# Down product of a feed-forward layer by seven block products, in a fused two-block Trainium2 kernel

## What is computed

```python
def conv_glu_ffn(h, w_up, conv_w, conv_b, w_down):
    u = causal_dwconv(h @ w_up, conv_w) + conv_b
    a, b = jnp.split(u, 2, axis=-1)
    return (jax.nn.silu(a) * b) @ w_down          # 1024x2816 by 2816x1024
...
        y = memory_cross_attention(rmsnorm(h, g[2]), ...)
        h = h + rmsnorm(y, g[3])
        y = conv_glu_ffn(rmsnorm(h, g[4]), ...)
        h = h + rmsnorm(y, g[5])
...
        mod = jax.nn.silu(c) @ w_ada[layer] + b_ada[layer]
        shift, scale, gate = jnp.split(mod[:, None, :], 3, axis=-1)
        h = rms_norm(x, norm_g[layer]) * (1.0 + scale) + shift
        proj = h @ w_in[layer]
```

## Time and profile before

| | us |
|---|---|
| three executions: median (lowest, highest) | 2670.04 (2668.05, 2671.69) |
| the profiled execution | 2670.99 |
| its span, first to last instruction | 2669.2 |
| PE busy | 2591.1 (97%) |
| DVE busy | 1659.6 (62%) |
| POOL busy | 1131.9 (42%) |
| ACT busy | 844.0 (32%) |

### The profile page before, as it was taken

How to read it: one execution, slowest core, us unless ns; L and a number is a source line. 1 busy time by engine, 2 the same in 40 slices (tenths; PEclk the granted TensorE clock), 3 DMA queues, 4 the chain that set the end, 5 groups by cost and what they waited for, 6 DMA issues and landing times.

```text
span 2669.2 us, 33144 instructions
## 1 busy us (share of the span) xinstructions
PE 2591.1 (97%) x13218; PEld 2174.4 (81%) x13218; DVE 1659.6 (62%) x2194; ACT 844.0 (32%) x1332; POOL 1131.9 (42%) x651
## 2 busy tenths in 40 slices
PE   6999899989999999999999999999999999999998
PEld 5788788877788777888888887888888888888887
DVE  4879978766512587666674558804555556476566
ACT  4011233334223433333332436212222222343342
POOL 2433100046632548777754444673223322242364
PEclk9999999999999999999999999999999999999999
DMA  4122333235312412222245553573333342466682
GB/s 153 56 94 97 99 124 127 95 104 206 112 62 79 158 58 86 79 87 79 87 149 191 169 178 121 186 258 106 134 111 111 130 147 94 159 251 211 223 315 111
DMA packets 147381, 360.25 MB, mean 135 GB/s; under 512 B 15173, under 2 KB 51229, under 8 KB 147100
## 3 DMA queue, kind: packets, MB, share of 16 engines
q1 hardware_dynamic: 65072, 177.81, 19.9%
q10 hardware_dynamic: 82156, 180.33, 18.9%
HBM read 268.90 MB, written 89.19 MB: 134 GB/s over the span
## 4 chain that ended last, share of the span: by engine, by line
PE 89%; DVE 4%; POOL 2%; ACT 2%; issue 1%; DMA 1%; ACTq 0%; POOLq 0%; DVEq 0%
PE pp L296 32%; PE pp L2213 13%; PE pp L494 11%; PE pp L2266 9%; PE pp L278 9%; PE pp L2953 2%; PE pp L1272 2%; POOL w_lo L3653 1%; PE pp L1944 1%; PE pp L1983 1%; POOL w_hi L3651 1%; DMA w_raw<-in_weights 1%; PE pp L1558 1%; PE pp L1597 1%; PE pp L444 1%
## 5 line engine op out<-in xcount | busy, mean ns | idle before, releaser
L3651 POOL CAST w_hi<-w_raw 128x1024 fp32r<-128x1024 f32 x184 | 222.2, 1207 | 990.3 <-PE pp L296 659.5
L296 PE MATMUL pp<-w_hi,act_hi 128*128 128x512 f32 x1344 | 535.9, 399 | 12.7 <-POOL w_lo L3653 9.9
L296 PE MATMUL pp<-w_lo,act_hi 128*128 128x512 f32 x1344 | 524.5, 390 | 0.0
L296 PE MATMUL pp<-w_hi,act_lo 128*128 128x512 f32 x1344 | 524.5, 390 | 0.0
L3653 POOL TENSOR_TENSOR w_lo<-w_raw,w_hi 128x1024 fp32r<-128x1024 f32 x184 | 468.9, 2549 | 14.7
L296 PEld LDWEIGHTS pp<-w_hi,act_hi 128*128 128x128 f32 x1344 | 253.0, 188 | 67.9 <-POOL w_lo L3653 10.8
L296 PEld LDWEIGHTS pp<-w_hi,act_lo 128*128 128x128 f32 x1344 | 252.6, 188 | 53.5
L296 PEld LDWEIGHTS pp<-w_lo,act_hi 128*128 128x128 f32 x1344 | 253.2, 188 | 48.3
L494 PE MATMUL pp<-act_hi,w_hi 128*128 128x512 f32 x480 | 192.7, 402 | 10.6 <-DVE act_lo L849 6.5
L2184 POOL TENSOR_TENSOR w_lo<-w_raw,w_hi 128x1024 fp32r<-128x1024 f32 x52 | 132.5, 2550 | 164.7 <-ACT w_hi L2178 164.6
L494 PE MATMUL pp<-act_lo,w_hi 128*128 128x512 f32 x480 | 190.5, 397 | 0.0
(11 more groups left out here) (468 smaller groups left out, 5282.9 us busy)
## 6 DMA issues: line engine op xcount, KB each, us to landing
w_raw<-in_weights SPq DMA_DIRECT2D x314, 512.0 KB, 3.5
z_s<-hg_st ACTq DMA_DIRECT2D x52, 512.0 KB, 4.1
hid_s<-ffn_cb ACTq DMA_DIRECT2D x22, 512.0 KB, 2.6
ffn_graw<-hid_s ACTq DMA_DIRECT2D x44, 256.0 KB, 3.1
hg_qkb<-hT_s SPq DMA_DIRECT2D x16, 512.0 KB, 8.1
qkvT_s<-mixin_o ACTq DMA_DIRECT2D x12, 512.0 KB, 2.8
gdn_qkv<-qkvT_s ACTq DMA_DIRECT2D x8, 768.0 KB, 6.4
front_x<-in_x ACTq DMA_DIRECT2D x8, 512.0 KB, 5.0
```

Of the source, the lines that this page charges most:

```text
L296: last = pe.matmul(dst, a[:, k, t * P:(t + 1) * P], columns(w, j, k, 0, n), start=(k == 0 and a is high and w is w_hi), stop=(k == NK - 1 ...
L3651: pool.tensor_copy(hi, raw).then_inc(w_split, 1)
```

## The change

The down product is now done on 2x2 blocks. The tokens are halved (rows of A), the 22 strips of the hidden dimension go in 11 pairs (columns of A, rows of B), and the 1024 columns of the weight are halved. In place of eight block products there are seven, some of them of sums: T1 to T4 of weight blocks, S1 to S4 of hidden blocks. Each takes 11 steps of 12 matmuls (now L2381), 77 steps in all.

```diff
-FCHUNKS = ((0, 1, 2, 3), (4, 5, 6, 7))
-N_DOWN = len(FCHUNKS) * FG
+DOWN = (("A11", "B11"), ("A12", "B21"), ("S2", "T2"), ("S1", "T1"), ("S4", "B22"), ("S3", "T3"), ("A22", "T4"))
+DOWN_HALVES = (FG + 1) // 2
+N_DOWN = len(DOWN) * DOWN_HALVES // 2
```

```diff
+            BY_DVE = 6
...
+            def store(self, act, k):
+                if k < self.BY_DVE:
+                    after(act, self.by_dve, "T4", k)
+                else:
+                    after(act, self.by_pool, "T4", k - self.BY_DVE)
+                act.dma_start(self.kept[k], self.bufs[k % 3][:, :, :]).then_inc(self.stored[k % 3], 16)
+
+            def make(self, eng, S, k, n):
+                b11, b12, b21, b22 = (self.bufs[k % 3][:, i, :] for i in range(4))
+                eng.wait_ge(self.loaded[k % 3], self.loaded_before + 16 * (k // 3 + 1))
+                S.done(eng.tensor_tensor(b11, b12, b11, ALU.subtract), "T1")
+                S.done(eng.tensor_tensor(b12, b22, b12, ALU.subtract), "T3")
+                after(eng, S, "T3", n)
+                S.done(eng.tensor_tensor(b22, b22, b11, ALU.subtract), "T2")
+                after(eng, S, "T2", n)
+                S.done(eng.tensor_tensor(b21, b21, b22, ALU.subtract), "T4")
...
+            def finish(self, act):
+                self.store(act, FG - 2)
+                self.store(act, FG - 1)
+                self.landed(act)
+
+            LOADS = {4: (0,), 5: (1,), 6: (2,), 10: (3,), 11: (4,), 12: (5,)}
+            STORES = {7: 0, 8: 1, 9: 2, 13: 3, 14: 4, 15: 5}
+            LATE_LOADS = {0: (6,), 1: (7,), 3: (8,), 6: (9,), 7: (10,)}
+            LATE_STORES = {4: 6, 5: 7, 7: 8}
```

```diff
+                def hidden_sums(k, *names):
+                    M, h = self.hs_made, T // 2
+                    a11, a21 = self.cb[0][:, 0:h], self.cb[0][:, h:T]
+                    a12, a22 = self.cb[1][:, 0:h], self.cb[1][:, h:T]
+                    s1, s2, s3, s4 = (self.hs[:, n, :] for n in range(4))
+                    if "S1" in names:
+                        after(dve, V, "g", 2 * k + 1)
+                        if k:
+                            dve.wait_ge(self.hs_stored, self.hs_before + 16 * k)
+                        M.done(tt(s1, a21, a22, ALU.add), "S1")
+                        M.done(tt(s3, a11, a21, ALU.subtract), "S3")
+                    if "S2" in names:
+                        after(dve, M, "S1", k)
+                        M.done(tt(s2, s1, a11, ALU.subtract), "S2")
+                        after(dve, M, "S2", k)
+                        M.done(tt(s4, a12, s2, ALU.subtract), "S4")
```

```diff
+                def down(n, u, frees=False):
+                    p, k = n // FG, n % FG
+                    j, i = half(n)
+                    w = [x[SLOT[PART_AT[j] + i]][:, k % 2 * WC:(k % 2 + 1) * WC] for x in (w_hi, w_lo)]
                     g = [self.piece(x, n) for x in (self.gh, self.gl)]
+                    fresh = DOWN[p][0] in ("A11", "S2", "S1", "S3")
                     for a, b in ((0, 0), (0, 1), (1, 0)):
-                        for h in range(2):
-                            last = pe.matmul(pp[u][:, h * 512:(h + 1) * 512], g[a][:, u * P:(u + 1) * P], w[b][:, h * 512:(h + 1) * 512],
-                                             start=(k == 0 and a == 0 and b == 0), stop=(k == FT - 1 and a == 1))
-                            if frees is not None:
-                                frees(last)
-                                frees = None
+                        last = pe.matmul(self.down_bank(p, u), g[a][:, u * P:(u + 1) * P], w[b], start=(fresh and k == 0 and a == 0 and b == 0),
...
+                def join(p, name):
+                    J, y, h = self.joined, self.y, T // 2
+                    for u in range(NT // 2):
+                        after(dve, self.down_made, "made", p * (NT // 2) + u)
+                        x, lo, hi = self.down_bank(p, u), y[:, NT // 2 + u, 0:h], y[:, NT // 2 + u, h:T]
+                        if name == "u":
+                            after(dve, self.kept, f"s{u}", 0)
+                        else:
+                            after(dve, J, f"u{u}" if name in "veg" else f"v{u}", 0)
+                        dst, a = {"u": (lo, y[:, u, h:T]), "v": (hi, lo), "e": (y[:, u, h:T], lo), "f": (hi, hi), "g": (lo, lo)}[name]
+                        J.done(tt(dst, a, x, ALU.add), f"{name}{u}")
```

```diff
+            FIRSTS = {56: 0, 58: 1, 60: 2, 69: 3}
+            KEEPS = {58: 0, 60: 1, 62: 2, 71: 3}
+            SECONDS = {62: 0, 67: 1, 71: 2, 74: 3}
+            TURNS = {64: 0, 69: 1, 73: 2}
+            HIGHS = {66: 0, 70: 1, 74: 2}
```

```diff
-                    for t in {1: (4,), 2: (5,), 3: (6, 7)}.get(j, ()):
+                    for t in {1: (4,), 3: (5,), 4: (6,), 5: (7,)}.get(j, ()):
...
                 sig(1)
+                sig(2)
                 R.high(act, 5)
                 R.second(act, 7)
                 self.prev.cast_down(act, N_DOWN * 2 + 4)
                 self.prev.cast_down(act, N_DOWN * 2 + 5)
-                sig(2)
+                sig(3)
                 R.high(act, 6)
                 R.high(act, 7)
-                sig(3)
```

More of the change, by code:

```diff
@@ L677, in act, with dve, taps @@
                         self.next.exps_of(act, self.EXPS[j])
-        def taps(dve, V, name, rnd, dst, src, w, n, bias=None, amid=None):
-            for j in range(n):
+                    if j in W.STORES:
+                        W.store(act, W.STORES[j])
+                    if j == NT // 2 + 2:
+                        after(act, R.N, "xn", NT - 1)
+                    for k in W.LOADS.get(j, ()):
+                        W.load(act, k)
+            def dve(self, dve):
+                W, S = self.sums, self.next
+                for k in range(4):
+                    W.make(dve, W.by_dve, k, k)
+                S.softmax_of(dve, 0)
+                W.make(dve, W.by_dve, 4, 4)
+                S.softmax_of(dve, 1)
+                W.make(dve, W.by_dve, 5, 5)
+        def taps(dve, V, name, rnd, dst, src, w, n, bias=None, amid=None, only=None):
+            for j in range(n) if only is None else (only,):
                 k = n - 1 - j
@@ L2388, in act, with first @@
                         self.cast(act, i + 1, "A12", "A22")
+                        if i == 0:
+                            store_sums(0)
+                        elif r % 2 == 0:
+                            store_sums(r // 2 - 1)
                     else:
                         cast_down(2)
-                for n in range(len(FCHUNKS) * FT):
-                    c, k = n // FT, n % FT
-                    if c and k == 0:
-                        for t in FCHUNKS[c - 1]:
-                            self.keep(act, t)
-                        after(act, self.kept, "kept", NT // 2 - 1)
+                def first(t):
+                    after(act, self.joined, f"e{t}" if t < NT // 2 else f"g{t - NT // 2}", 0)
+                    N_.first(act, t)
@@ L2397, in act @@
+                after(act, self.prods, "p3", SEVEN - 1)
+                load(4)
+                load(5)
+                for n in range(self.STEPS):
+                    p, k = n // FG, n % FG
                     high(n + 2)
-                    cast_down(n + 3)
-                    load(n + 4)
+                    if k % 2 == 0:
+                        cast_down(p * DOWN_HALVES + k // 2 + 3)
+                    load(n + 6)
                     if n == 1:
                         silu(FT - 1)
-                    elif n == 3:
+                    elif n == 6:
@@ L2419, in act @@
+                    if n in self.KEEPS:
+                        N_.second(act, self.KEEPS[n])
+                    if n in self.FIRSTS:
+                        first(self.FIRSTS[n])
+                    if n in self.HIGHS:
+                        N_.high(act, self.HIGHS[n])
+                N_.high(act, 3)
                 first(4)
-                self.keep(act, 5)
-                N_.high(act, 0)
                 first(5)
-                self.keep(act, 6)
-                N_.high(act, 1)
@@ L3639, in _ @@
                     continue
[L3640 to L3641 removed]
+                if FIRST_STRIP["down"] <= j < FIRST_STRIP["hf_hq"]:
+                    continue
+                if FIRST_STRIP["hf_hq"] <= j < FIRST_STRIP["hf_hq"] + HI_BY_ACT:
+                    for i in range(2):
+                        ffn.split_half(pool, 2 * (j - FIRST_STRIP["down"]) + i)
                     continue
                 for i in range(HALVES[j]):
+                    if j == FIRST_STRIP["o"] + 1 and i == 0:
+                        xq.sums.pool(pool)
                     r, q = RAW_AT[j] + i, PART_AT[j] + i
```

351 lines of the change are left out of this document (228 added, 123 removed).

## The result

| | us |
|---|---|
| the changed kernel, median of 4 executions (lowest, highest) | 2695.36 (2694.41, 2698.22) |
| before, median of 4 beside them | 2670.6 (2668.05, 2671.69) |
| ratio, 95% interval | 1.0101 (1.0089 to 1.0114) |
| span of its profiled execution | 2694.0 |

A forecast was written before the change was run, and what follows sets the result against it. TensorE, busy for 97% of the span, was taken to bound the kernel. Down's -32.0 us and added waits, clock losses and VectorE work summed to +9.7, giving 2679.7 us, range 2656 to 2697.

The forecast's parts named there:

- The matmuls: Down product: 924 matmuls, 209.5 us, plus four turns, 3.2, make 212.7, which is 32.0 us less.
- I cost this at nothing: Down product: VectorE, ScalarE and weight loads at 193 GB/s fit in each two steps; costed at nothing.
- rival 3: Down product becomes bound by its feeding, 38 steps late by 0.5 us: +19 on the forecast, 2699; chance 0.11.
- Nothing: Norm rows in separate steps and row stores ahead of their norm: same transfers, spread; costed at nothing.
- HgInputs: Stage after down: TensorE waits 10.8 at job 4, 7.1 at job 6, 1.5 at job 2, less 2.9: +16.5.
- the clock: HgInputs: TensorE runs at its lower clock level after the longer waits; +4.5 us (0 to 7).
- The rest: Everything after HgInputs to the start of the kernel's last matmul; forecast to change by 0.
- Attention: GpSimd's sums of blocks 6 and 8 hold up VectorE's operations on p: +5.5 us, and 1.5 for the clock.
- Rival 1: Faster: engines don't hold each other up and HgInputs' waits are short; -6.8 us, 2663; chance 0.30.
- a reading by which L2107 is left alone: Attention: VectorE's short operation on p takes no shared-port lock, so the term would be 0, not 5.5.
- xo: Stage xo: unit 4 waits for ScalarE's keep behind the last store, and for GpSimd's splits; +6.5, clock 2.2.
- up_seven: Seven products of up: VectorE's added 128x512 operations delay splits where it is already late; +5 us (1 to 9).

The follow-up runs named there:

- e7: Changed kernel with row transfers and norm operations of the down product's last-step tiles cut to 128 of 1024 columns; 2685.14 us, down 213.1.
- e5: The changed kernel, unaltered, run again as a measure for other runs; 2691.41 us, ratio 1.0091.
- e6: Changed kernel with norm operations of tiles 0 to 3 in down cut to 128 of 1024 columns, transfers untouched; 2685.97 us, down 216.1.
- e4: Changed kernel with GpSimd's sums of weight blocks 6 to 10 cut to 4 of 512 columns, loads and stores kept; 2681.9 us.
- e9: Changed kernel with HgInputs' four casts early, all weight sums on VectorE in Queries, and norm of tiles 0 to 3 spread; 2657.9 us, ratio 0.9963.

## Why the prediction was right or wrong

- **The matmuls**: 212.7 us were worked out, 213.1 measured (e7). Right.
- **"I cost this at nothing"** (the feeding of down): wrong, and this is the step that failed. It weighed the feeding by a mean of two steps, VectorE some 2.7 us of 5.44, and 193 GB/s, and such a mean held: for 158 us TensorE lost 0.2 us at 226 GB/s. The term put at nothing measured 14.7 us, 11.2 in e5, with what the lower clock took in that stretch. It left out the norm of four tiles: before, it lay over eleven strips, some 60 us, while GpSimd did the splits; now it lies over the last 21 steps, 57 us, and the splits and twice as many activation pieces stand with it in the same rows of VectorE and ScalarE. e6 and e7 show that norm operations and row transfers together are worth all of it, 10.8 us on e5's execution, 14.3 on the first. For rival 3, to which I gave 0.11, I named the right place in the wrong extent: 38 steps late by 0.5, where TensorE stands three times in the last 20 steps, for 1.9 to 4.8 us. The sentence "Nothing" on the norm's separate steps is where the text should have counted them.
- **HgInputs**: waits of 10.8 and 7.1 forecast, 10.77 and 7.07 measured; with job 2 and less the old waits 16.4, where the sum had 16.5. The stage lost 17.5, so the clock cost 1.1 and not the 4.5 of the forecast. Part of the low stretch fell on time in which TensorE stood anyway: in 1650.1 to 1655.6 the granted clock is 0.50 and no matmul runs.
- **The rest**, which the forecast left at nothing, lost 4.3. Of these 3.1 lie in the first strip behind HgInputs. The ring of weight slots runs on from stage to stage, and the down product now uses 42 halves of it and not 44, so HgInputs' last strip lies in the slots that the next stage needs for its third and fourth half. GpSimd's cast of the third half, before and then in the change (TensorE starts the stage at 1800.17 and 1820.69):

```profile
1796.52 1.53 POOL L3651 CAST w_hi<-w_raw 128x1024 fp32r<-128x1024 f32 x1 [2.04 <-DMA w_raw<-in_weights]
```

```profile
1821.21 1.04 POOL L3872 CAST w_hi<-w_raw 128x1024 fp32r<-128x1024 f32 x1 [4.87 <-PE pp L297]
```

  TensorE waits 3.3 us for splits there, 0.5 before. In every run of the changed code this cast comes 0.5 us behind the stage's start, and the strip loses 3.1 us or more. This is read from the code and the traces; no run undoes it. The other 1.2 lie near the end and differ by execution.
- **Attention**: +7.0 against +9.3 (e5: 7.0). The step was right, and e4 shows that it is GpSimd's operations alone. The waits are 5.9 us over those of before, where the sum had 5.5; the other 3.4 are the clock's, to which it gave 1.5. That e5's total meets the forecast is partly luck, as the same code took 4.1 to 9.3 over before. Rival 1, by which VectorE isn't held up, had 0.30 and is out: L2107 took up to 1.44. The forecast named a reading by which L2107 is left alone and the term 0; the trace goes against it. It isn't the page's own reading either: the Trainium skill's "SBUF — State Buffer", section "Who interferes with whom", counts tensor_scalar among the operations that can enter a two-port mode, and the 4.45 us agree with that.
- **xo**: +8.7 against +12.9. The chain was right (loads and stores of 1 MB landed after 5.8 and 4.7 us in the median, and from the last `act_hi` to the keep it was 20.9 us, where I had 18.7 to 21.2; the terms as written add up to 18.1 to 20.4), and TensorE's wait was 5.3 against 3 to 5. Mis-sized is what follows: TensorE stood another 3.6 for GpSimd's splits, so the waits were 8.9 and not 6.5, and the other 4.1 are the clock's, to which the sum gave 2.2. e4 shows that the wait for the splits does not go with the sums.
- **up_seven**: +5 against +3.5, inside its bounds.
- **The start**: attention began 4.4 us earlier than before, in e5 4.6, but in e4 and e6, whose code up to there is the same, 1.0 and 0.7. It differs by execution, and no run ties it to the change.

Sum of the table: -4.4 + 9.3 + 12.9 - 1.0 + 3.5 - 17.3 + 17.5 + 4.3 = 24.8. The forecast sum was 9.7, so 15.1 lie beyond it. Down is 14.7 of these; the other terms miss by 4.2, 2.3 and 4.3 upwards (xo, attention, the rest) and by 4.4, 1.0, 1.5 and 3.5 downwards (start, the stage ahead of up_seven, up_seven, HgInputs), which nearly cancel. In e5 the span is 18.4 longer than before, 8.7 beyond the sum, and down is 11.2 over its term: there too it is the largest miss.

## What to carry to other kernels

A change that takes matmuls from a stage must be costed where most other work stands beside them, not at the stage's mean: follow one round of each ring of buffers (load, land, cast, split) with everything that stands between on the in-order engines, and compare with the time TensorE leaves for it. Spreading that work within the same 21 steps bought little (1.7 us, e9); its amount is what counted. See what each cast waits for: before, it was a free slot, which is margin; in the change it was mostly the load, and each further delay came closer to the matmuls. If the change uses a ring of buffers a different number of times, look at where the ring stands for the stage that follows. Where one engine's row of steps holds both the operands of the next job and steps that wait for something late, put the operands first: four casts moved were worth 19 us here. And an engine that is idle on average may be the wrong place for work, if it holds up a short operation on another one's critical path.
